# A hybrid decode step on one core: ScalarE's cached-attention exponentials put ahead of its value-page loads

## What is computed

```python
k_past = cache_k[j][page_table].reshape(db, past_len, KV_HEADS, HEAD_DIM)
v_past = cache_v[j][page_table].reshape(db, past_len, KV_HEADS, HEAD_DIM)
...
logits = jnp.einsum('bqhd,bqhsjd->bqhsj', qi, kg) * scale
logits = jnp.where(mask, logits, -jnp.inf).reshape(b, qc, ATT_HEADS, -1)
p = jax.nn.softmax(logits, axis=-1).reshape(b, qc, ATT_HEADS, ksel + 1, MOBA_BLOCK)
return jnp.einsum('bqhsj,bqhsjd->bqhd', p, vg)
```

## Time and profile before

| what | us |
|---|---|
| median of three runs | 2016.27 |
| the profiled execution | 2013.78 |
| its span, first to last instruction | 2012.0 |
| TensorE busy | 1863.8 |
| VectorE busy | 1315.1 |
| ScalarE busy | 940.8 |

### The profile page before, as it was taken

One profiled execution on the slowest core, in us unless ns is written; L12 is line 12 of the kernel. 1 busy time (PEld: TensorE's weight loads), 2 busy tenths in 40 slices (PEclk: granted clock), 3 DMA queues, 4 the chain that ended last, 5 costly groups with the idle time before them and its releaser, 6 DMA issues.

```text
span 2012.0 us, 27307 instructions
## 1 busy us (share of the span) xinstructions
PE 1863.8 (93%) x10177; PEld 1536.4 (76%) x10177; DVE 1315.1 (65%) x1359; ACT 940.8 (47%) x824; POOL 76.8 (4%) x94
## 2 busy tenths in 40 slices
PE   6999798899999973888999999999999999999996
PEld 4788783799998741366888888888888888888885
DVE  5863874454543231123887878879889788787894
ACT  3542000244431031012776767767677667676772
POOL 1340303000000000000000000000000000000000
PEclk8997795999999996796999999999999999999998
DMA  6222003355445789961998989989989899897980
GB/s 278 105 91 84 1 1 149 133 189 187 172 175 211 220 307 387 339 272 70 361 366 326 342 313 362 354 318 342 352 319 346 318 351 352 319 347 311 360 334 23
DMA packets 96731, 512.34 MB, mean 255 GB/s; under 512 B 10769, under 2 KB 10898, under 8 KB 44418
## 3 DMA queue, kind: packets, MB, share of 16 engines
q1 hardware_dynamic: 81936, 478.50, 63.2%
q10 hardware_dynamic: 13970, 25.46, 3.5%
q0 software_dynamic: 736, 7.21, 1.0%
HBM read 503.91 MB, written 7.21 MB: 254 GB/s over the span
## 4 chain that ended last, share of the span: by engine, by line
issue 65%; PE 28%; DVE 4%; ACT 1%; DMA 0%; SPq 0%; POOLq 0%; POOL 0%; ACTq 0%; DVEq 0%
PE bank L487 5%; PE bank L488 5%; PE bank L489 5%; PE bank L786 3%; PE bank L720 2%; PE bank L698 1%; PE bank L599 1%; PE bank L643 1%; PE bank L623 1%; PE bank L636 1%; DVE w_lo L1388 1%; PE bank L481 1%; ACT w_hi L1047 1%; DVE scr L1444 0%; PE bank L508 0%
## 5 line engine op out<-in xcount | busy, mean ns | idle before, releaser
L1755 DVE TENSOR_TENSOR w_lo<-raw_w,w_hi 128x2048 fp32r<-128x2048 f32 x336 | 768.6, 2290 | 140.7 <-ACT w_hi L1213 137.3
L1213 ACT ACTIVATE w_hi<-raw_w 128x2048 fp32r<-128x2048 f32 x336 | 644.9, 1920 | 369.6 <-PE bank L955 279.8
L953 PE MATMUL bank<-w_hi,xe_hi 128*128 128x512 f32 x896 | 365.1, 407 | 1.5 <-DVE xe_lo L1813 1.5
L955 PE MATMUL bank<-w_hi,xe_lo 128*128 128x512 f32 x896 | 350.5, 391 | 0.0
L954 PE MATMUL bank<-w_lo,xe_hi 128*128 128x512 f32 x896 | 349.9, 390 | 0.0
L488 PE MATMUL bank<-fh_lo,w_hi 128*128 128x264 f32 x704 | 201.6, 286 | 0.0
L953 PEld LDWEIGHTS bank<-w_hi,xe_hi 128*128 128x128 f32 x896 | 168.9, 189 | 35.9 <-issue 1.8
L955 PEld LDWEIGHTS bank<-w_hi,xe_lo 128*128 128x128 f32 x896 | 168.7, 188 | 36.2
L954 PEld LDWEIGHTS bank<-w_lo,xe_hi 128*128 128x128 f32 x896 | 168.9, 189 | 33.8
L953 PE MATMUL bank<-w_hi,aT_hi 128*128 128x512 f32 x448 | 176.9, 395 | 0.0
L954 PE MATMUL bank<-w_lo,aT_hi 128*128 128x512 f32 x448 | 174.5, 389 | 0.0
(11 more groups left out here) (328 smaller groups left out, 2362.7 us busy)
## 6 DMA issues: line engine op xcount, KB each, us to landing
raw_w<-in_moe SPq DMA_DIRECT2D x336, 1024.0 KB, 4.8
raw_w<-in_ffn_w SPq DMA_DIRECT2D x42, 1024.0 KB, 4.8
ring<-in_k_pages SPq DMA_DIRECT2D x96, 256.0 KB, 3.5
raw_w<-in_gdn_in SPq DMA_DIRECT2D x16, 1024.0 KB, 5.4
ring<-in_v_pages SPq DMA_DIRECT2D x64, 256.0 KB, 11.6
ring<-in_v_pages ACTq DMA_DIRECT2D x64, 256.0 KB, 11.3
ring<-in_att_in SPq DMA_DIRECT2D x4, 2048.0 KB, 7.9
ring<-in_k_pages ACTq DMA_DIRECT2D x32, 256.0 KB, 7.5
```

The costliest lines, as they stand in the source:

```text
L953: mm(out, hi, move_hi, start=first, stop=False)
L955: return mm(out, lo, move_hi, start=False, stop=last)
L1213: A(w_hi[:, p % SPLIT, :], raw_w[:, p % RAW, :], ACT.Copy).then_inc(split_hi, 1)
L1755: V.tensor_tensor(w_lo[:, p % SPLIT, :], raw_w[:, p % RAW, :], w_hi[:, p % SPLIT, :].bitcast(F32), ALU.subtract).then_inc(split_lo, 1)
```

## The change

ScalarE's list is put in another order. The loop over V1 to V7 before the exponentials now runs over `range(C_V + 1, C_V)`, which is empty. After the exponentials ScalarE issues its four pages of V1. After the two copies of the probabilities it issues its pages of V2 to V15 in one go. V0 is issued where it was, in the loop over the heads. The instructions, their number and the waits of each load are the same; SP's list, TensorE's and VectorE's are not touched.

```diff
-            for n in range(C_BOTH + H + 1, C_V + SLOTS):
+            for n in range(C_BOTH + H + 1, C_V):
                 load_pages(act, n, range(PPC // 2, PPC))
             act.wait_ge(bias_done, 1)
             for n in range(BLOCKS):
                 A(prob[:, 256 * n:256 * (n + 1)], bank[n // 2][:, 256 * (n % 2):256 * (n % 2 + 1)], ACT.Exp,
                   bias=biases[:, n:n + 1], scale=SCALE, accum_out=sums[:, n:n + 1])
             A(p_new, l_new, ACT.Exp, bias=m_neg, scale=SCALE).then_inc(pexp, 1)
+            for n in range(C_V + 1, C_V + 2):
+                load_pages(act, n, range(PPC // 2, PPC))
             for i in range(2):
                 act.wait_ge(probT_ps, i + 1)
                 A(prob_T[:, 8 * i:8 * (i + 1), :].rearrange("p g r -> p (g r)"), bank[4 + i][:, :], ACT.Copy)\
                     .then_inc(probT_sb, 1)
-            for n in range(C_V + SLOTS, C_AOUT):
+            for n in range(C_V + 2, C_AOUT):
                 load_pages(act, n, range(PPC // 2, PPC))
```

## The result

The changed kernel took 2025.59 us (median of five, 2023.36 to 2027.71) beside 2016.27 for the kernel before: ratio 1.0048, 95% interval 1.0033 to 1.0062, that is 9.7 us slower (6.7 to 12.5). The forecast was 2026.3. The profiled execution took 2024.42, its span 2022.5. All ratios here leave out two executions that took more than twice the usual time, 4666 us in four_first and 6359 us in the kernel before.

The account below looks back on a forecast made before the run. The value phase was taken as bound by DMA bytes. The last value chunk at +11.0 us, less 0.8 for the att_out wait, gave +10 us on 2016.3: forecast 2026.3, range 2016 to 2036.

Parts of the forecast that it names:

- Part 1: Exponentials on ScalarE go ahead of page issues, start at 776.6, and all hung on them moves 20.2 us earlier.
- Part 2: ScalarE's 56 later page issues run from 789.6, none waiting for a slot, the last at 847.4 as before.
- Rival (b): No change: last page issued at 847.4 and landing at 860 to 862 behind the old queue; 2015 to 2017, chance 0.11.
- the cover that "just holds": Pages queued at the DMA engines while ScalarE is silent: 2 left at 780.6, 1 at 789.6; 2 us lost at worst.
- rival (d): DMA runs dry before 789.6, or one queue alone cannot fill the engines: +20 us and more, 2037, chance 0.06.
- Rival (c): ScalarE's pages served first or SP held back by slots: V15 at 855.9, -6 us, 2010.3, chance 0.06.
- The sum in bytes: Value phase: 95 pages left at 789.5 end at 853.9, landing adds 2.0: floor 855.9, a gain of 6.2 us.
- Step 1: SP ends its value pages at 842.3 with 17 of ScalarE's left; att_out loads are queued before that.
- Step 2: att_out's 16 KB packets alternate with ScalarE's 2 KB ones until 853.5; ScalarE gets 2 pages, 15 left.
- Rival (a): Queues share bytes, not packets: ScalarE's last page lands at 867.4, +4.5 us, 2020.8, chance 0.17.
- Step 3: Expert loads reach the engines at 861.5 with 3 ScalarE pages left, alternate to 871.1; V15 lands at 873.1.
- The sum: +11.0 us for the last value chunk, -0.8 for the att_out wait, cold clock taken as 0: +10 us.

Follow-up runs that it names:

- four_first: Changed kernel with ScalarE's halves of V1 to V4 issued before the exponentials, V5's after them, V6 to V15's after the copies: ratio 0.9982 to before.
- hold_both: Changed kernel with SP waiting until V14 is read before issuing the two att_out loads, expert pieces behind them: ratio 0.9985 to before.
- small_packets: Changed kernel with each att_out chunk loaded as eight DMAs of 256 KB in 2 KB packets instead of one of 2 MB in 16 KB packets: ratio 1.0075 to before.
- hold_experts: Changed kernel with one more wait on SP: the first seven expert pieces wait until all 16 value chunks are read: ratio 1.0017 to before.
- three_first: Changed kernel with ScalarE's halves of V1 to V3 issued before the bias wait, V4's after the exponentials, V5 to V15's after the copies: ratio 0.9990 to before.
- three_dense: three_first with one more wait on TensorE, which takes V12 only when V14 has landed: ratio 0.9992 to before.
- two_first: Changed kernel with ScalarE's halves of V1 and V2 issued before the bias wait, V3's after the exponentials, V4 to V15's after the copies: ratio 1.0079 to before.
- sp_takes_two: Changed kernel with SP issuing all pages of V1 and V2, and ScalarE none between V0's and the copies, then V3 to V15's: ratio 1.0102 to before.

## Why the prediction was right, step by step

- **Part 1** held to the microsecond: exponentials at 775.82 (said 776.6, with the keys 0.75 us earlier here), chunk 0 at 788.84 (789.6).
- **Part 2, the last issue at 847.4**, was wrong: it went out near 859.7. The sum ignored that issues can be held up. While att_out moved, single issues of ScalarE took up to 5.0 us (median 0.34). The stall itself cost no bytes: from 855 to 864 the DMA engines moved 387 to 389 GB/s, so an earlier issue of the last page would only have put it behind the same pages sooner. Rival (b) rested on this instant being the old one, and on the old queue behind it; both are gone, as the page issued at 840 took 17.5 us to land.
- **The DMA engines stay full**: from 790 to 840 they moved 386 GB/s on the mean; the cover that "just holds" held, and the first ground of rival (d) with it is out. Rival (c) needed att_out to be held back to about 850; it was issued at 835.
- **The sum in bytes**: hold_both shows the floor, V15 taken at 858.2 where 855.9 was said. The windows of hold_both, in the order of the earlier trace rows, tell a part of the 2.3 us more:

```profile
845.00:850.00 5.00, 4.76 (x36) 1.58 (x28) 0.17 (x1) 0.00 (x0) 0.00 (x0) 0.84 1.05 387
850.00:855.00 5.00, 4.76 (x40) 1.80 (x40) 0.64 (x2) 0.00 (x0) 0.00 (x0) 1.00 0.94 332
```

From 845 to 850 ScalarE's queue moves alone, and at 387 GB/s: one queue of 2 KB packets fills the engines while it has pages waiting, so the second ground of rival (d) is out as well. Then it runs low, with a page issued only every 1.05 us; 55 GB/s short over 5 us is 0.7 us. No run took the rest apart.

- **Step 1**: att_out at 835.45 and 839.15 where 833 and 838 were said.
- **Step 2**: alternation packet by packet, ScalarE at 0.23 MB of 2.10, 11%. Rival (a) is excluded by that row, and small_packets shows that the packet's size is the cause. The rule of the Trainium skill, "DMA: Bandwidth & Descriptors", section "Queues, rings and completion order", points the right way; it speaks of a packet of about 9 to 17 descriptors drained in one go. The counts by half-microseconds above (9 to 18 of ScalarE's packets in each) do not fit bursts of eight, which is all that a page gives an engine, and so not that number: here the turns were single.
- **Step 3** was the term of V15 that was mis-sized most. The 2 us to an expert piece's first byte, which no row gave, were 1.3 (issued at 861.22, first packet at 862.56). When that packet moved, ScalarE had 1.8 pages left to send and not three. Only its last page landed late, by 4.5 us against the same page in hold_experts, and not by 9.6. V15 was taken at 870.87 where 873.1 was said.
- **The terms of V15**, counted from the end of the last key chunk: the forecast has 84.2 for the floor (855.9), 9.8 for att_out (to 865.7) and 7.4 for the experts (to 873.1), together 101.4. Hold_both and hold_experts give 86.5, 9.6 and 3.8, together 99.9. So the att_out term was right, and the two others missed by 2.3 and 3.6 us in opposite directions.
- **The sum**: +11.0 for V15 was +9.5. The tail to the projection, said to shrink by 0.8 with the clock taken as nothing, grew by 1.9: the last chunk (3.64 for 1.92) and `turn_o` (1.86 for 1.05) ran at the low clock. The projection, said to shift whole, grew by 1.3 from the same cause. The prediction had named a changed stretch behind 867 as a sign of being wrong, and in this term it was. So V15 was over-sized by 1.5, and what follows it under-sized by 2.7 + 1.3 = 4.0, nearly all of it the clock; the measured span (+10.5) is close to the +10 because the 0.75 us at the keys and the 1.3 us of the experts' phase went the other way: 10 - 1.5 + 4.0 - 0.75 - 1.3 = 10.5. The mechanism and the att_out term are borne out; that the sum came within a microsecond is in part luck, as errors of up to 4 us cancelled.

What stays open is that 1.3 us. It is there in hold_both, three_first and three_dense (1.3 to 1.6), and not in hold_experts, small_packets, two_first, four_first or sp_takes_two (at most 0.4); each is one execution.

## What to carry to other kernels

An engine's idle gap beside full DMA engines is worth only the bytes that closing it lets move sooner; here 20 us of waiting were worth 6.2 by the forecast, and the most that any order got for V15 was 3.9 (hold_both). When loads that gate the next step are moved to a later place in one queue, count what the other queue will issue in the meantime, and in what packets: a queue of 16 KB packets takes eight ninths from one of 2 KB. Either hold the later loads behind a wait on the gating ones, or see to it that the queue with the small packets finishes first. Four_first does the second and is 0.18% (0.06 to 0.30) faster than before; hold_both does the first, and the two can't be told apart.

## What the runs showed of the hardware

- Two queues fed by SP and ScalarE take turns by packet whatever their size: 1.93 to 1.93 MB with equal packets, 0.23 to 1.87 with 2 KB against 16 KB, 0.75 to 3.36 against 8 and 16 KB. The turns are single packets (9 to 18 of either queue in every half-microsecond from 842 to 850.5 of the changed kernel).
- One queue of 2 KB packets alone moved 387 GB/s (hold_both, 845 to 850), as much as two together.
- An issue can hold up its engine: up to 5.0 us for one of 0.34. Every value-page issue of ScalarE's that took over 1 us had 10 or 11 pages of its queue under way, which looks like a queue that is full; no run tested this. In the stretch of before where issues began to be held up, at 785 to 790, a page took 14.1 us to land; at half of 1.476 pages per us that is about ten pages of one queue under way.
- The same 48 products of the projection took from 10.92 to 13.69 us in the ten kernels, by how long they ran at 1.2 GHz before the clock rose to 2.4. They began low after sparse chunks in the changed kernel (its last chunk took 3.64 us for 1.92), and in hold_both after two chunks at the high clock and an idle wait of 3.04 us (granted share 0.50 from 865 to 870). In the windows the granted share was 1.00 over hold_experts' projection (870 to 902) and 0.91 over that of the changed kernel (877 to 912). This can add to a gain in the sparse phase before it (hold_experts, 3.8 us and 2.5 more) or take some of it (three_first).
